# GpSimd instead of VectorE subtracts for most rests in an output projection of split float32 products

## The reference

```python
o_l = jnp.concatenate([a_l, b_l, c_l, d_l], axis=-1) @ w_out
x_l = x_l + mod_l[2] * rms_norm(o_l, norm_post_mix[layer])
h = modulate(rms_norm(x_l, norm_pre_ffn[layer]), mod_l[3], mod_l[4])   # the input of conv_ffn
```

## Time and profile before

| | before |
|---|---|
| median of 3 runs | 4455.67 us (4452.32 to 4456.72) |
| profiled execution, span | 4452.7 us (its own time is not listed apart; the fastest run shown took 4452.32 us) |
| TensorE busy | 3870.9 us (87%) |
| VectorE busy | 2075.6 us (47%) |
| ScalarE busy | 1338.9 us (30%) |
| GpSimd busy | 1050.2 us (24%) |
| mean granted TensorE clock | 0.934 of full speed |
| projection of layer 0 with its norms | 1276 to 1449 us of the span |
| projection of layer 1 with its norms | 3546 to 3699 us of the span |

### The profile page before, as it was taken

How to read it: one execution, slowest core, us unless ns; L and a number is a source line. 1 busy time by engine, 2 the same in 40 slices (tenths; PEclk the granted TensorE clock), 3 DMA queues, 4 the chain that set the end, 5 groups by cost and what they waited for, 6 DMA issues and landing times. The chain is left out here.

```text
span 4452.7 us, 80728 instructions
## 1 busy us (share of the span) xinstructions
PE 3870.9 (87%) x33188; PEld 3116.4 (70%) x33188; DVE 2075.6 (47%) x2860; ACT 1338.9 (30%) x1835; POOL 1050.2 (24%) x834
## 2 busy tenths in 40 slices
PE   6999569678888999999997999569679889999997
PEld 3888445466766888888885888345567677888886
DVE  3464755565547332232235244755556563232234
ACT  5121333233334312211225222333243333222223
POOL 1000510004521322332332000510016313233233
PEclk9999679799998999999998999679789989999998
DMA  4444130100012111111120334130100121111112
GB/s 189 163 156 163 61 117 1 30 27 3 4 61 85 48 38 36 35 33 42 36 74 26 120 125 147 54 114 1 30 28 4 36 90 57 47 47 47 47 47 94
DMA packets 72136, 285.77 MB, mean 64 GB/s; under 512 B 8000, under 2 KB 11328, under 8 KB 66880
## 3 DMA queue, kind: packets, MB, share of 16 engines
q1 hardware_dynamic: 55744, 201.53, 13.1%
q10 hardware_dynamic: 16128, 80.49, 5.0%
HBM read 226.67 MB, written 47.45 MB: 62 GB/s over the span
## 5 line engine op out<-in xcount | busy, mean ns | idle before, releaser
L3297 DVE SCALAR_TENSOR_TENSOR y<-ps,taps,y 128x1023 f32<-128x1023 f32 (+1 forms) x132 | 134.2, 1016 | 865.1 <-DVEq L3295 857.9
L497 PE MATMUL ps<-h_hi,wu_hi 128*128 128x512 f32 x1680 | 460.0, 371 | 9.6 <-PEq L3197 9.6
L497 PE MATMUL ps<-h_hi,wu_raw_rest 128*128 128x512 f32 x1680 | 459.5, 371 | 0.0
L497 PE MATMUL ps<-h_whole_rest,wu_hi 128*128 128x512 f32 x1680 | 459.0, 371 | 0.0
L3389 POOL TENSOR_TENSOR wu_raw_rest<-wu_raw,wu_hi 128x1024 fp32r<-128x1024 f32 x84 | 201.3, 2396 | 1031.3 <-POOLq L3388 1031.3
L497 PE MATMUL ps<-h_hi,w_hi 128*128 128x512 f32 (+1 forms) x1200 | 313.8, 366 | 35.2 <-PEq L493 35.2
L497 PEld LDWEIGHTS ps<-h_hi,wu_hi 128*128 128x128 f32 x1680 | 294.5, 188 | 66.0 <-issue 9.9
L497 PEld LDWEIGHTS ps<-h_hi,wu_raw_rest 128*128 128x128 f32 x1680 | 294.8, 188 | 56.3
L497 PEld LDWEIGHTS ps<-h_whole_rest,wu_hi 128*128 128x128 f32 x1680 | 294.2, 188 | 56.2
L497 PE MATMUL ps<-h_whole_rest,w_hi 128*128 128x512 f32 (+1 forms) x1200 | 311.9, 364 | 0.0
L497 PE MATMUL ps<-h_hi,w_raw_rest 128*128 128x512 f32 (+1 forms) x1200 | 311.8, 364 | 0.0
(11 more groups left out here) (411 smaller groups left out, 7694.4 us busy)
## 6 DMA issues: line engine op xcount, KB each, us to landing
wu_raw<-in_w_up_dram SPq DMA_DIRECT2D x88, 512.0 KB, 3.2
w_raw<-in_w_in_dram SPq DMA_DIRECT2D x54, 512.0 KB, 4.7
ada_w<-in_ada_rest_dram ACTq DMA_DIRECT2D x27, 1024.0 KB, 6.1
rows<-rows ACTq DMA_DIRECT2D x42, 640.0 KB, 4.7
wd_raw<-in_w_down_dram SPq DMA_DIRECT2D x40, 512.0 KB, 4.1
h_whole<-rows SPq DMA_DIRECT2D x24, 640.0 KB, 6.7
ada_w<-in_ada_rest_dram ACTq DMA_DIRECT2D x27, 512.0 KB, 4.9
wd_raw<-in_w_out_dram SPq DMA_DIRECT2D x16, 512.0 KB, 3.3
```

Of the source, the lines that this page charges most:

```text
L497: mm = pe.matmul(ps[:, lo:lo + width], w[a][:, t, :], rhs[b][:, t, lo:lo + width], start=(t == 0 and i == 0), stop=(t == n_k - 1 and i == 2))
L3297: dve.scalar_tensor_tensor(y[:, s, lo + 1:hi], ps[s][:, lo:hi - 1], k.taps[:, s, 0:1], y[:, s, lo + 1:hi], ALU.mult, ALU.add).then_inc(own ...
```

## The change

The number `early` = 4 parts the loads. The rests of loads 0 to 3 stay on VectorE; those of loads 4 to 15 go to GpSimd, each right after that load's CAST. The rests of the mixers' outputs of segment 0 stay on VectorE; those of segments 1 and 2 go to GpSimd. GpSimd's queue becomes a loop over the 24 instances: at each, the CAST and the rest of the load that is first used three instances later (if there is one), then one rest of the mixers' outputs of the next segment. TensorE waits for two new marks, `w_lo_pool` and `o_lo_pool`, where the work moved. The arithmetic and the DMAs are the same.

```diff
--- before.py
+++ after.py
@@ -3100,6 +3100,8 @@
         w_in = [k.mark(f"out_w_in{q}") for q in range(4)]
         w_hi_done, w_lo_done, o_hi_done, o_lo_done, out_done, evicted, spilled = (
             k.mark(m) for m in "w_hi_done w_lo_done o_hi_done o_lo_done out_done evicted spilled".split())
+        w_lo_pool, o_lo_pool = k.mark("w_lo_pool"), k.mark("o_lo_pool")
+        early = 4
         ref = Refresh(k, segs, orders, 2, 3, 4, mixed,
                       sq1, sq2, acc1, acc2, r1, r2, sums)
         sq1_done, x_added, lo_done = k.mark("sq1_done"), k.mark("x_added"), k.mark("lo_done")
@@ -3461,12 +3463,18 @@
             @block.tensor
             def _(pe):
                 for i, (s, p, t) in enumerate(instances):
-                    pe.wait_ge(w_lo_done.sem, w_lo_done.at(load_of[i] + 1))
+                    if load_of[i] < early:
+                        pe.wait_ge(w_lo_done.sem, w_lo_done.at(load_of[i] + 1))
+                    else:
+                        pe.wait_ge(w_lo_pool.sem, w_lo_pool.at(load_of[i] - early + 1))
                     if i >= 4:
                         pe.wait_ge(sq1_done.sem, sq1_done.at(i - 3))
 
                     def halves(u):
-                        pe.wait_ge(o_lo_done.sem, o_lo_done.at(8 * s + u + 1))
+                        if s:
+                            pe.wait_ge(o_lo_pool.sem, o_lo_pool.at(8 * (s - 1) + u + 1))
+                        else:
+                            pe.wait_ge(o_lo_done.sem, o_lo_done.at(u + 1))
 
                     segment_products(pe, place_of(i), (w_hi[t % 4], w_lo[t % 4]), (k.hi, k.o_lo), cols(s), KD,
                                      halves if p == 0 else None).then_inc(out_done.sem, 1)
@@ -3596,7 +3604,7 @@
                 rest_w(2)
                 for i, (s, p, t) in enumerate(instances):
                     ref.add1(dve, s, p)
-                    if i + 3 in fresh:
+                    if fresh.get(i + 3, early) < early:
                         rest_w(fresh[i + 3])
                     if s and p == 2:
                         dve.wait_ge(evicted.sem, evicted.at(8 * s))
@@ -3617,8 +3625,6 @@
                     if s >= 2 and 2 <= p <= 6:
                         for u in range(max(2 * p - 5, 0), min(2 * p - 3, KD)):
                             ref.lower(dve, s - 2, u)
-                    if s < last:
-                        rest_o(s + 1, p)
                 dve.wait_ge(evicted.sem, evicted.at(end))
                 dve.wait_ge(out_done.sem, out_done.at(end))
                 for u in range(KD + 2):
@@ -3688,10 +3694,26 @@
                     pool.sem_inc(own["pool"], -1)
                     pool.sem_inc(wu_pe[s], 1)
 
-                for j in (0, *range(4, len(loads))):
-                    weights(j)
+                def rest_w(j):
+                    q = loads[j][0] % 4
+                    pool.wait_ge(w_hi_done.sem, w_hi_done.at(j + 1))
+                    pool.tensor_tensor(w_lo[q], w_raw[q], w_hi[q].bitcast(F32), ALU.subtract).then_inc(w_lo_pool.sem, 1)
+
+                def rest_o(s, t):
+                    pool.wait_ge(o_hi_done.sem, o_hi_done.at(8 * s + t + 1))
+                    pool.tensor_tensor(k.o_lo[:, t, cols(s)], k.oT[:, t, cols(s)], k.hi[:, t, cols(s)].bitcast(F32),
+                                       ALU.subtract).then_inc(o_lo_pool.sem, 1)
+
+                weights(0)
+                for i, (s, p, t) in enumerate(instances):
+                    j = fresh.get(i + 3, 0)
+                    if j >= early:
+                        weights(j)
+                        rest_w(j)
                     if j == 7:
                         first_up(0)
+                    if s < last:
+                        rest_o(s + 1, p)
                 first_up(1)
                 pool_group(pool, 0, first=True)
                 with pool.Fori(0, N_FG // 2 - 1) as i:
@@ -3717,7 +3739,8 @@
         if layer < DEPTH - 1:
             for m, count in ((xsq_done, KD), (xpart_done, KD), (xln_done, 1), (xroot_done, 1)):
                 m.base += count
-        for m, count in ((w_hi_done, len(loads)), (w_lo_done, len(loads)), (o_hi_done, end), (o_lo_done, end),
+        for m, count in ((w_hi_done, len(loads)), (w_lo_done, early), (w_lo_pool, len(loads) - early),
+                         (o_hi_done, end), (o_lo_done, KD), (o_lo_pool, end - KD),
                          (out_done, end), (evicted, end), (spilled, 16 * (last + 1))):
             m.base += count
```

## The result

The changed kernel takes 4466.77 us (median of 9 runs, 4461.70 to 4470.19), the kernel before 4455.67 us (9 runs beside it, 4451.44 to 4457.42). The ratio is 1.0029, with a 95% interval of 1.0021 to 1.0037: 9 to 16 us slower (the medians differ by 11.1 us). 4470.9 us had been forecast, with a range of 4458 to 4478.

The account below looks back on a forecast made before the run. VectorE was taken to bound the projections from instance 10 until the norms are done. Segment terms 2.65 + 2.76 + 6.17 + 3.61 = +15.2 us gave a span of 4467.9, plus 3 us for the median: 4470.9 us, range 4458 to 4478.

Parts of the forecast that it names:

- VectorE is the limit from instance 10 on: In the projections, VectorE's queue sets the pace from instance 10 until the norms are done.
- GpSimd holds VectorE's two-tensor instructions, CASTs too: While GpSimd subtracts or casts, VectorE instructions with both tensors in SBUF stand still; those reading PSUM don't.
- The price of a moved rest: Where VectorE is the limit, each moved load's rest costs 1.27 us; where VectorE was waiting, nothing.
- Segment 0: 0: In segment 0 of both layers the moved work costs nothing; GpSimd and VectorE together need 35 of 40 us.
- The terms by segment: Losses in segments 1 and 2: layer 0, 2.65 and 2.76 us; layer 1, 6.17 and 3.61 us.
- The mixers' rests: 0 but for the last two: In segment 1 of each layer, moved mixers' rests fall into VectorE's waits, except the last two, costing 0.96 us.
- The work after segment 2 starts later by the sum: Last parts of the norms and feed-forward part keep their work; first y about 5 us later, then 15 in layer 1.
- The other signs: Many VectorE instructions in segments 1 and 2 end 0.5 us after GpSimd's L3700, which take 2.4 to 3.5 us.
- TensorE's waits for the weights go, and nobody gains: In segment 2, TensorE's waits for weight rests vanish, but its wait at L2961 grows beyond 9.8 us.
- 1 (side by side): GpSimd works beside VectorE, holding it less than 1.13 us per subtraction: 12.4 us of relief, 4443 us; chance 8%.
- 2 (mostly covered, +6.4): GpSimd's work falls into VectorE's waits in segment 1; only segment 2 pays, 6.4 us: 4462 us; chance 14%.
- 3 (GpSimd the limit in layer 1): GpSimd limits layer 1's segment 1; up to some 7 us hidden, beyond that say 8 us more: 4479; chance 6%.

Follow-up runs that it names:

- e3: Kernel before with the rests of loads 9 to 11 and 13 to 15 left out, TensorE reusing the rounded weights: 12.5 us faster than before (8.5 to 16.5).
- e1: Changed kernel with the mixers' rests given back to VectorE, only the loads' rests on GpSimd: 6.2 us slower than the kernel before (2.2 to 10.2).
- e10: Kernel before; second first-up load in VectorE's gap, six loads' roundings on ScalarE behind its squares, their rests behind VectorE's additions to x: 4438.02 us, ratio 0.9959.
- e2: Changed kernel with all loads' rests back on VectorE, only the mixers' rests on GpSimd: 2.2 us slower than the kernel before (-1.8 to 6.2).
- e6: Kernel before with the roundings of loads 9 to 11 and 13 to 15 on ScalarE, ahead of eviction and square: 6.2 us slower (2.2 to 10.2).

## Why the prediction was right, point by point

- **VectorE is the limit from instance 10 on.** Right: e3 takes 12 rests off it and gets 12.5 us back, 1.0 us for each (15.0 us by the profile).
- **GpSimd holds VectorE's two-tensor instructions, CASTs too.** Right, by the turns in segment 2, by e1 against e3, and by e10, where the stretching is gone with the instructions.
- **The price of a moved rest, 2.40 - 1.13 = 1.27 us.** Wrong in size. It measured 2.0 - 1.1, some 0.9 us. This is the term of the sum that was mis-sized: it stands in it 11 times, 11 x 0.37 = 4.1 us too much. Of these, 1.25 us had been taken off already, as waits that cover a part in the two segments 2 (the measured price has its waits in it), so 2.8 to 4.1 us. I had taken GpSimd's duration as the length of the hold; what holds is that duration less some 0.3 us.
- **Segment 0: 0.** Right: the segment's last addition stands 50.8 and 49.3 us after the start in the two profiles of before, 50.0 and 49.3 us in those of after.
- **The terms by segment.** At the last addition, the means of two profiles each. Layer 0, segment 1: 96.6 to 97.8, +1.2 (forecast 2.65). Segment 2: 143.3 to 146.1, another +1.6 (2.76). Layer 1, segment 1: 85.8 to 90.5, +4.8 (6.17). Segment 2: 126.4 to 133.6, another +2.5 (3.61). Together +10.1 in place of 15.2; the price above is 2.8 to 4.1 of these 5.1 us. In layer 0 the two profiles of before differ by 1.4 us at the end of segment 1, so the first two of these values are uncertain by as much; from instance 18 on, where pairs of profiles agree within 0.1 us, segment 2 costs 2.6 us in layer 0 and 2.8 in layer 1, against 2.76 and 3.61. In layer 1's segment 1 the loads' rests alone make 2.7 us (e1; forecast 5.2) and the mixers' rests alone 2.0 (e2; forecast 0.96), so one term was too high there and one too low.
- **Additivity of the segments.** Not quite. Layer 0's lateness of 1.2 us is down to 0.3 at instance 18 (107.7 and 108.0 us), as VectorE waits there for ScalarE's squares (6.06 us before, 5.50 after) and these for TensorE, which isn't late. From there on it grows again, by 2.6 us.
- **The mixers' rests: 0 but for the last two, 0.96 us in each layer.** In the sum the runs of e2 fit (2.2 us, -1.8 to 6.2, where 1.9 was forecast). By the profile it is 0.1 us, made of 1.9 us less in layer 0 and 2.0 more in layer 1; the cause of this is open.
- **The work after segment 2 starts later by the sum.** By a little less: of 10.1 us at the last addition, 8.6 arrive at the first y (8.9 and 8.2). The sign given for this, the first y 5 us later in layer 0 and 15 in layer 1, came out at 2.0 and, both layers together, 8.6.
- **The other signs.** VectorE's stretched instructions end 0.55 us after GpSimd's (1386.22 and 1386.77, 1390.47 and 1391.02), as said. GpSimd's L3700 take 2.39 to 2.73 us; none takes the 3.5 that was allowed for.
- **TensorE's waits for the weights go, and nobody gains.** Right in segment 2, where the waits of 5.6 us in layer 0 and 6.3 in layer 1 went into L2961 (9.8 to 18.0, 6.5 to 12.5 us). In layer 1, at instances 14 to 16, TensorE waits for GpSimd's rests in place of VectorE's, and longer: 4.0, 2.7 and 3.0 us where it was 0.8, 3.2 and 2.4.
- **Rivals.** 1 (side by side) is excluded: it asked for a faster kernel, and GpSimd's subtraction holds VectorE for 2.0 of its 2.40 us, where the rival needed less than 1.13. 2 (mostly covered, +6.4) lies below the interval of both measurements, 9.4 and 8.0 us, though as a mechanism it has its part in the +1.2 of layer 0's segment 1. 3 (GpSimd the limit in layer 1) shows its beginnings in TensorE's waits: instance 15 begins 79.2 us after the start in place of 73.8, within the 7 us that the rival itself called hidden, and segment 1 came out below the forecast, not above.
- **The number.** 4470.9 against 4466.8. The span of 4467.9 that the sum gave meets the profiled 4468.3, but by luck: the terms were 5 us too high at the last addition and 6.6 at the first y, and that profile had 6.3 us of scatter between the projections. The timed runs say 12.9 and 12.0 us where the projections explain 8.6, and what the rest is stays open; so the nearness of 4466.8 is in part luck too. The upper edge of 4477 is 1 to 2 us more than the two terms given for it (4.2 and 0.3 us) add up to.

## What to carry to other kernels

Before moving work from VectorE to an idle GpSimd, look at where VectorE is the limit and at the operands: if both engines' tensors lie in SBUF, GpSimd's busy time, less some 0.3 us an instruction, is added to VectorE's queue. So where VectorE is the limit, the move pays only if that is less than the instruction takes on VectorE; here it was 2.0 us against 1.1. In such stretches the opposite paid here: take GpSimd's own work out, to ScalarE or into a wait of VectorE, and place it in ScalarE's queue behind what VectorE waits for. The roundings in the wrong place of ScalarE's queue (e6) lost by the runs as much as the loads' half of the change did, 6.2 us.

## What was not expected of the hardware

- In segment 2 of layer 0 the two engines alternate strictly, one instruction each, in a cycle of 4.25 us for 3.44 us of GpSimd's work and 1.41 us of VectorE's: 4.85 us of work in 4.25 us, so about 0.3 us per GpSimd instruction overlap after all.
- Two profiled executions of one kernel differed by 6.7 us in a stretch of 2092 us that runs the same instructions (2091.7 and 2098.4 us), but only by 0.3 us over a projection. A difference of spans is to be split by stages before it is explained.
